# A limit of four row gathers under way in GpSimd's expert loop

## The reference

```python
def token_block(xt):
    q = (xt @ wq).astype(f32).reshape(PEER_TOKEN_BLOCK, PEER_HEADS, 2, PEER_DKEY // 2)
    s = jnp.einsum('thcd,hckd->thck', q, sub_keys.astype(f32))
    top_s, top_i = lax.top_k(s, PEER_TOPK)
    ...
    expert = i1 * PEER_NKEYS + i2
    w = jax.nn.softmax(best_s, axis=-1)
    act = jax.nn.gelu(jnp.einsum('thkd,td->thk', u[expert].astype(f32), xt.astype(f32)))
    return jnp.einsum('thk,thkd->td', w * act, v[expert].astype(f32))
```

## Time and profile before

| | us |
|---|---|
| median of 3 executions without a profile | 1531.32 |
| lowest, highest | 1529.78, 1531.53 |
| span of the profiled execution | 1607.1 |
| first and last gather issued, in the profiled execution | 201.37, 956.87 |
| loop that the change touches | 266.09 to 956.87 |

### The profile page before, as it was taken

The page is one execution under the profiler, slowest core; times in us unless marked ns, Lnnn a source line. Parts: engine busy times, 40 slices in busy tenths (PEclk is TensorE's granted clock), DMA queues, the critical chain, the costliest instruction groups (busy, mean ns, idle before and its releaser), DMA issues.

```text
span 1607.1 us, 16314 instructions
## 1 busy us (share of the span) xinstructions
PE 1394.8 (87%) x5950; PEld 935.5 (58%) x5950; DVE 1048.3 (65%) x1860; ACT 587.4 (37%) x908; POOL 516.5 (32%) x554
## 2 busy tenths in 40 slices
PE   8999967876876678777777779999999999999998
PEld 7965666322332223222233337888888898688887
DVE  4646679555656556655646567677898466679873
ACT  4553221221111111111112316874665356456652
POOL 4000046666666666666667750000000000000000
PEclk9999998988988988987788899999999999999999
DMA  9532379899999999999999995424565464355642
GB/s 301 189 105 92 111 299 400 313 353 370 361 383 358 361 366 361 371 373 374 355 367 378 365 349 198 158 105 157 160 207 185 157 210 158 105 179 188 208 166 99
DMA packets 162751, 413.69 MB, mean 257 GB/s; under 512 B 11249, under 2 KB 57579, under 8 KB 162544
## 3 DMA queue, kind: packets, MB, share of 16 engines
q0 software_dynamic: 75664, 272.63, 45.0%
q1 hardware_dynamic: 86832, 139.94, 25.6%
q10 hardware_dynamic: 176, 0.07, 0.0%
HBM read 411.56 MB, written 1.05 MB: 257 GB/s over the span
## 4 chain that ended last, share of the span: by engine, by line
PE 66%; issue 12%; POOL 6%; DMA 5%; DVE 4%; another core or an unknown queue 3%; ACT 3%; DVEq 0%; SPq 0%; ACTq 0%
PE ps L1352 19%; PE ps L1516 9%; PE ps L1536 7%; PE ps L854 7%; PE ps L1524 5%; POOL arena L3294 3%; DMA ring<-in_peer_v,routes 2%; PE ps L1211 1%; PE ps L1507 1%; PE ps L1255 1%; PE ps L1239 1%; POOL ring L3305 1%; PE ps L1269 1%; PE ps L1279 1%
## 5 line engine op out<-in xcount | busy, mean ns | idle before, releaser
L2823 DVE SCALAR_TENSOR_TENSOR arena<-arena,ps 128x1024 f32<-128x1024 f32 x256 | 306.2, 1219 | 197.7 <-DMA arena<-in_peer_u,routes 155.4
L3294 POOL DMA_INDIRECT arena<-in_peer_u,routes x256 | 247.4, 966 | 116.7 <-issue 73.7
L2054 ACT ACTIVATE state<-cst,gatew 128x128 f32<-128x128 f32 x236 | 86.0, 396 | 476.2 <-remote 206.1
L1352 PE MATMUL ps<-ring,state 128*128 128x512 f32 x308 | 167.5, 676 | 80.0 <-issue 70.4
L2386 DVE TENSOR_TENSOR w_lo<-ring,w_hi 128x2048 fp32r<-128x2048 f32 x66 | 151.0, 2290 | 71.8 <-ACT w_hi L2201 71.8
L1352 PEld LDWEIGHTS ps<-ring,state 128*128 128x128 f32 x308 | 60.4, 210 | 177.5 <-issue 177.0
L1516 PE MATMUL ps<-x_both,w_hi 128*128 128x512 f32 x640 | 160.3, 393 | 0.0
L2201 ACT ACTIVATE w_hi<-ring 128x2048 fp32r<-128x2048 f32 x66 | 125.9, 1911 | 68.2 <-PE ps L1536 49.8
L1352 PE MATMUL ps<-mixed,state 128*128 128x512 f32 x156 | 95.7, 759 | 41.5 <-issue 30.9
L1516 PEld LDWEIGHTS ps<-x_both,w_hi 128*128 128x128 f32 x640 | 115.2, 189 | 20.5
L1352 PE MATMUL ps<-wX,state 128*128 128x512 f32 x156 | 81.6, 665 | 26.5 <-issue 24.9
(11 more groups left out here) (547 smaller groups left out, 2516.9 us busy)
## 6 DMA issues: line engine op xcount, KB each, us to landing
ring<-in_ffn_w_up SPq DMA_DIRECT2D x22, 2048.0 KB
ring<-in_ffn_w_down SPq DMA_DIRECT2D x10, 2048.0 KB
ring<-in_even_w_in SPq DMA_DIRECT2D x7, 2048.0 KB
ring<-in_w_in SPq DMA_DIRECT2D x6, 2048.0 KB
ring<-in_odd_w_in SPq DMA_DIRECT2D x6, 2048.0 KB
ring<-in_peer_wq SPq DMA_DIRECT2D x3, 2048.0 KB
ring<-in_w_out SPq DMA_DIRECT2D x2, 2048.0 KB
arena<-in_peer_u,routes POOLq DMA_INDIRECT x256
```

The lines of the kernel that those rows point to most:

```text
L1352: last = mm(ps[:, 4 + 2 * (u // PAIR_UNITS) + half_, :], diags[n % DIAGS], v_slots[value_slot(u, b)][:, 512 * half_:512 * half_ + 512], st ...
L2054: do(diags[n % DIAGS], ident, ACT.Copy, scale=gatew[:, u * UROWS + b:u * UROWS + b + 1]).then_inc(diag_ready, 1)
L2823: v.scalar_tensor_tensor(row, row, 1.0, token_tile(u // PAIR_UNITS), ALU.mult, ALU.mult, accum_out=dots[:, b:b + 1]).then_inc(u_used, 1)
L3294: pool.indirect_dma_start(arena[:, b % GATHER_SLOTS, :], None, a["peer_u"][0], route_of(u, b))\
```

## The change

In the double loop two waits of POOL are added; nothing is taken out and nothing is reordered. From the third row of a unit on, `gather_u(u + 1, b)` is issued only when row b - 2 of the same unit of u has landed, and `gather_v(u, b)` only when value row b - 2 has. Since rows of u and of v alternate, this is in both cases the gather four places back in POOL's own order. There is no such wait in the first two rows of a unit (four gathers of 64), in the 32 gathers ahead of the loop, and in the last unit, where only value rows are gathered. So 7 times 60, 420 gathers of 512, carry the new wait.

```diff
@@ -3314,11 +3314,15 @@
                     pool.wait_ge(idx_ready, u + 2)
                 for b in range(UROWS):
                     if u + 1 < UNITS:
+                        if b > 1:
+                            pool.wait_ge(u_landed[(b - 2) % GATHER_SLOTS], 16 * ((b - 2) // GATHER_SLOTS + 1 + (u + 1) * (UROWS // GATHER_SLOTS)))
                         gather_u(u + 1, b)
                     if (u, b) == (0, len(query_rows)):
                         pool.wait_ge(sk_done, UNITS - TT)
                     if (u, b) == (0, len(query_rows) + 1):
                         pool.wait_ge(sk_done, UNITS)
+                    if u + 1 < UNITS and b > 1:
+                        pool.wait_ge(*value_landed(u, b - 2))
                     gather_v(u, b)
```

## The result

| | before | changed |
|---|---|---|
| median of 4 executions, us | 1530.57 | 1650.11 |
| lowest, highest, us | 1529.78, 1531.53 | 1648.3, 1652.46 |
| span of the profiled execution, us | 1607.1 | 1646.5 |

One of the changed kernel's four executions, the one of 1648.3 us, is the profiled one; the profiled execution of the kernel before is none of its four. The changed kernel is slower by 119.5 us, a ratio of 1.078 with a 95% interval from 1.0767 to 1.0793. The direction was forecast, the size was not: 1576.7 us was predicted, with a range from 1530 to 1622.

A forecast was written before the change was run, and what follows sets the result against it. The prediction took DMA transfers as the bound, 1.275 us a gather, POOL close behind. 378 gathers x (1.40 - 1.28) = 45 us on 1531.3 gave 1576.7 us, range 1530 to 1622.

The forecast's parts named there:

- Transfers are the bound, and a slower pace comes through one for one: Expert loop: a gather lands each 1.275 us, POOL issues each 1.24; slower landings lengthen the whole time equally.
- The pauses are something the profiled execution adds; 615 us for an unprofiled loop: Expert loop: 690.8 us profiled less 75.8 of pauses absent from unprofiled executions, 1.284 us a gather.
- The rival with real pauses: Expert loop: deep queue makes pauses in unprofiled executions too, the limit ends them; 1500 or 1473 us; chance of faster 0.14.
- A satisfied wait costs nothing: POOL's 420 added waits: one already satisfied adds no time, as gathers waiting for two semaphores keep 1.24 us spacing.
- 5.2 gathers are under way, so the limit acts: Long runs of the loop before: 6.5 us from issue to use over 1.24 us spacing, more than the limit of four.
- The pace is (L + 0.28) / 4: Limited loop: four gathers take one landing time plus 0.28 us wake-up; forecast 1.40 us a gather, at least 1.275.
- L: Landing time of a gather from its issue with four under way in the loop, taken as 5.31 us.
- the far end: Slowest end for the limited loop: landing time 6.22 us, 1.63 us a gather, 132 us lost.
- 54 of 64 gathers pay: Each unit: ten gathers at its start keep the full rate, 54 run slow, 7 x 54 = 378 in all.
- The loop that still saturates: Rival, limited loop: landing time falls to 4.82 us, transfers stay the bound, 1531 us; no change or a few us, chance 0.17.
- Transfers of 1.21 us a gather before the change: Unprofiled loop before: transfers at the 435 GB/s ceiling, POOL's 1.24 us sets the pace, loss would be 60 us.
- the rival with starved engines: Limited loop: landing time 6.2 us, pace 1.63 us, 1663 us (1622 with 5.8 us); chance of above 1603 us 0.15.

The follow-up runs named there:

- the second profile: The kernel before, unchanged, profiled a second time: 1531.23 us, ratio 1.0009, with a profiled span of 1529.9 us.

## Why the prediction was wrong, point by point

- *Transfers are the bound, and a slower pace comes through one for one.* Right: 409 GB/s without a pause, and 118.5 us of the 119.5 lie between the loop's ends. With half the bytes only 10 us are gained, so the bound is a close one.
- *The pauses are something the profiled execution adds; 615 us for an unprofiled loop.* Right for the sum: the second profile has no pauses, and its loop takes 877.4 - 259.3 = 618 us. The rival with real pauses is refuted. But profiling as such doesn't make them either, since no other profile here has them.
- *A satisfied wait costs nothing.* Right: 364 of them, ratio 1.0001.
- *5.2 gathers are under way, so the limit acts.* The conclusion was right, the number wrong: nine. In the trace I read, transfers went on through each pause while POOL issued almost nothing, so the queue kept on being emptied. It changed nothing in the sum, but it should have warned me that the trace showed no settled loop.
- *The pace is (L + 0.28) / 4.* Right, and with two or three in place of four it holds as well, with half the bytes too.
- *L.* **This is the step that failed.** I took 5.31 us, from the 395 GB/s of the stage 266 to 278, and called it a loop with about four under way. It was not: no gather waited there for a landing, POOL issued one each 1.24 us, and the transfer engines still had work from gathers issued ahead of the pause (408 GB/s from 266 to 269, as soon as POOL began again). A rate over 12 us beside an open queue is no landing time. The runs showed L = 6.0 us in its place. The rows behind the pauses were the better ones. The one with four gathers issued since the pause gave 6.22 us, 0.2 above the 6.0 measured, and I had left it for the far end because its transfer engines began empty. That it comes so near is in part luck: five more gathers were issued before it landed, so this wasn't a loop of four either. By my counting of gathers, the mis-sized term is 378 x (1.57 - 1.40) = 64 us of the 73 that were missing.
- *54 of 64 gathers pay.* Wrong by six: no ten gathers run at the full pace at a unit's start. The fifth gather already waits for the first, and the waits added to a unit's first rows cost only what the others do. With all 60 that carry the wait, 7 x 6 = 42 more pay, 42 x 0.29 = 12 us. The total alone couldn't tell: by the formula 54 give 112 us, 60 give 124, and 119.5 lies between.
- *The rivals.* The loop that still saturates needed a landing time of 4.82 us; even with two under way it is 5.0. The rule of the Trainium skill, page "DMA: Bandwidth & Descriptors", section "Latency and other measured facts", that a lighter load makes the fixed cost smaller, is not contradicted, but it is far too weak to save that rival: the landing time fell only from 6.0 to 5.0 us when the load was cut from 341 to 203 GB/s. Transfers of 1.21 us a gather before the change are refuted as well: the second profile, as long as the other executions, moves 409 GB/s. The time measured lies near the rival with starved engines (1663 us), to which I gave too little.

Together the predicted 45 us and the two corrections make 45 + 64 + 12 = 121 us, against 119.5 measured.

## What to carry to other kernels

A limit on transfers under way costs nothing as long as the limit times the transfers' pace is longer than landing time plus wake-up; below that, each transfer costs (landing + wake-up) / limit, and one waiting stream of two closes the loop nearly as well as both do (101 and 109 us against 119.5). Take the landing time at the new depth from transfers that are really issued at that depth, not from a rate beside an open queue, and leave a place or two of slack: at the computed minimum of five 17 us were still lost, at six 6. Profile the base kernel twice when its profiled span is far from its unprofiled time.

## What was unexpected of the hardware

- A 512 KB gather of 128 rows that has one other beside it lands after 5.0 us, and one of 256 KB after 3.4 us. Of the 5.0 us, 1.8 to 3.2 are transfer by the estimates above, more than the 1.275 us that a gather costs in a full queue. Two gathers under way give 203 GB/s, four 341, five 400, six 407, and no limit at all 409.
- The busy share of the DMA engines was 0.94 at 339 GB/s and 1.03 at 409 GB/s: it fell by 9% where the rate fell by 17%.
- One profiled execution held pauses of all engines at once, 76 us in sum, that a second profile of the same kernel doesn't show; the profiled spans of all the other kernels here are within 6 us of their medians. What made the pauses is open.
